# Latent-attention scores of a three-part block: the non-rotary product of each head made from rounded high parts and remainders instead of full float32 operands

## The chip, the cores and the metric

The kernel runs on one core of one Trainium2 chip. Its time is the device time of one execution in microseconds (us). The four compute engines named below are TensorE (PE; its weight loads are listed as PEld), VectorE (DVE), ScalarE (ACT) and GpSimd (POOL). SyncE (SP) only issues transfers here.

## The reference, cut to what matters

Two layers of a first block are followed by one layer of a second block, all in float32, for 256 tokens of width 2048. In each of the two layers a normed input is multiplied by `w_in` and split. Of the parts, `q_lat` (512 wide) is normed and multiplied by `w_uq`, `kv_lat` (256 wide) is normed and multiplied by `w_ukv`. For each of 8 heads this gives a query of 128 plain and 64 rotary columns, a key of 128 plain columns (the 64 rotary ones are shared by the heads) and a value of 128 columns. Then

```python
q = concatenate([q[..., :128], apply_rope(q[..., 128:], cos, sin)])
k = concatenate([k_nope, broadcast(k_pe)])
sc = einsum('bqhd,bkhd->bhqk', q, k) * 192 ** -0.5
p = softmax(sc); o = einsum('bhqk,bkhd->bqhd', p, v)
```

The rest of the layer is a gated short convolution, an attention of 4 heads over 256 memory tokens, a SiLU gate over all three, the product with `w_o`, a norm and a residual sum. The second block is a modulated Fourier mix and a squared-ReLU network of width 8192. The change touches only the product of the plain 128 columns of `q` and `k`.

## The kernel before, in words

**Two kinds of product.** Every large product is made from three rounded products. A float32 weight is split by ACT into a rounded high part (`whi`, type float32r, `split_hi`, L449 to L456) and by DVE into the remainder (`wlo`, `split_lo`, L458 to L463); the activations are kept in the same two parts, and PE adds high by high, high by remainder and remainder by high into PSUM (`fm_half`, `tm_half`, `ukv_half`, `pair_of`). All matmuls are written by `mm` at L467. The smaller products (scores, probabilities by values) have plain float32 operands in the kernel before, the rotary part of the MLA scores excepted: that has a rounded query of which both 64-row halves, high part and remainder, stand in one tile `qr`, against `krh` and `krl`.

**Steps.** The weights of a layer come in 1 MB units, and one half of a unit is a step; a layer has 144 steps. A step of a group is what PE does with one `whi` and one `wlo` tile. The groups in order are: memory keys and values (steps 0 to 15), `qlat` (16 to 23), `kvlat` (24 to 31), `gc` (32 to 39), four groups `uq` of two heads each and of 2 steps each (40 to 47), four groups `ukv` likewise (48 to 55), `xin` (2 groups of 4 steps, 56 to 63), `gb`, `qmem`, eight of `gate`, four of `wo`. Below, "uq2" is the third group of `uq`.

**Order on the engines.** PE, ACT and DVE each run through the steps in a fixed order of their own. At step s, ACT first rounds the weights of step s + 3 (AHEAD = 3), and DVE first makes their remainder. DVE next does one unit of the `w_mod` sum (L1160) where the plan of `mod_slots` has one: in this stretch at steps 43, 47, 50, 53 and from 57 on. Then both engines take the results of the group that PE has just ended out of PSUM (`ended`, ACT from L796, DVE from L1235). That is done at the step that follows the group's last: uq0 at step 42, uq3 at 48, ukv0 at 50, ukv3 at 56.

**Accumulators.** There are two PSUM accumulators of 1024 columns, used by turns (`acc_of`). The first matmul of a group therefore waits until the group two before it has been taken out: on the count `acc_act` for groups that ACT reads and `acc_dve` for those in the list `DVE_READS` (L82; PE waits from L1775 on).

**A group of `uq` before.** Columns 0 to 511 of the accumulator are the plain parts of two heads, columns 512 to 767 the rotary parts. ACT copies the rotary columns in four pieces to `swap` (L825), then the plain ones to `O` (L827), then rounds the rotary part of the previous group (`rotary_hi`, L794, L795; for uq0 the shared key part, L792). DVE multiplies the rotary columns by the cosines (the last time that it reads the accumulator, and where `acc_dve` is counted), then `swap` by the sines, adds the two, and makes the remainder of the previous group's rotary part (`rotary_lo`).

**A group of `ukv` before.** ACT copies the values to `V` (L830) and the plain keys of two heads to `kn` (L835). DVE does nothing with the accumulator; at ukv0 it makes the last rotary remainder.

**Scores.** Head h is scored before PE's share of step 59 + 3h (`QK_AT`). For each of two blocks of 128 queries, PE issues one float32 matmul `O` by `kn`, then `qr` by `krh` and `qr` by `krl`. The maximum, the exponential, the transposes and the product with the values follow at this and the next six steps, on DVE, ACT and PE.

**Memory.** `swap` lies at A + 38 KB, inside the 8 KB of `kn` (A + 32). So ACT waits, before it writes the keys of ukv3, until DVE has finished with `swap` (L833).

The lines that cause the wait at the head of a group:

```python
of = max(g - 2, 0)
if of in ACT_READS:
    pe.wait_ge(acc_act, act_reads(l, of))
if of and of in DVE_READS:
    pe.wait_ge(acc_dve, dve_reads(l, of))
```

Of the kernel before, what the change touches and what calls it, by code (L numbers as in the profile page):

```python
# [5 lines left out]
F32 = mybir.dt.float32  # L6
# [63 lines left out]
def acc_of(g):  # L70

    return (g + 1) % 2
# [6 lines left out]


ACT_READS = [g for g in range(NG) if GROUPS[g][1] != "FP"]
DVE_READS = [g for g in range(NG) if GROUPS[g][0] in ("mem", "uq", "wo") or GROUPS[g][1] == "FP"]  # L82
PAIRED = [g for g in range(NG) if GROUPS[g][1] == "FP"]


# [166 lines left out]
def build_program(nc, x, memt, positions, small, w_in, w_uq, w_ukv, w_mk, w_mv, w_o, post_g,  # L252
# [3 lines left out]
    with ctx:  # L256
        origin = nc.sbuf_base + (-nc.sbuf_base) % 64

        def at(name, shape, kb, dt=F32):
            return nc.alloc_sbuf_tensor_at(name, shape, dt, offset=origin + int(kb * 1024))  # L260
# [26 lines left out]
        csx = at("csx", [P, MT, SEQ], A + 36)  # L287
        otok = at("otok", [P, MT, D], A + 12)
        qpe = at("qpe", [P, HEADS // 2, SEQ], A + 28)
        kn = at("kn", [P, HEADS, SEQ], A + 32)  # L290
        qn = at("qn", [P, MT, QL], A + 32)
        kvn = at("kvn", [P, MT, KVL + 2 * ROPE], A + 36)
        swap = at("swap", [P, SEQ], A + 38)


        qr = at("qr", [P, HEADS, SEQ], 32, F32R)
# [422 lines left out]
        def _(act):  # L719
# [77 lines left out]
            def ended(act, l, g):  # L797

                name = GROUPS[g][0]
                a = acc[acc_of(g)]  # L800
                i = g - G_OF[name]
                act.wait_ge(half_used, l * LH + H_AT[g + 1])
                if name == "mem":
                    for t in range(MT):
                        factor = sc[:, RS + t:RS + t + 1] if l else 1.0
                        w = nc.scalar.activation(mv[:, t, :], a[:, t * 512:(t + 1) * 512], ACT.Copy, scale=factor)
                    w.then_inc(acc_act, 1)
                if name in ("qlat", "kvlat"):
                    w, n = (0, QL) if name == "qlat" else (1, KVL)
                    for t in range(MT):  # L810
                        i = nc.scalar.activation(sqlat[:, t, 0:n], a[:, t * 512:t * 512 + n], ACT.Square, scale=n ** -0.5,
                                                 accum_out=sc[:, LS + 2 * w + t:LS + 2 * w + t + 1])
                    i.then_inc(lat[w]["ss"], 1)
                if g in PAIRED:
                    if name == "gate" and i >= 2:
                        act.wait_ge(x_sum, 8 * l + i - 1)
                    if name == "qmem":
                        act.wait_ge(conv_out, 2 * l + i + 1)
                    nc.scalar.activation(xhalf[acc_of(g)][:, :, :], a.rearrange("p (t e n) -> p t e n", t=2, e=2)[:, :, 1, :],
                                         ACT.Copy).then_inc(x_copied, 1)  # L820
                if name == "uq":

                    act.wait_ge(rope_out, l * 5 + i + 1)
                    for b in range(4):
                        w = nc.scalar.activation(swap[32 * b:32 * b + 32, :], a[32 * (b ^ 1):32 * (b ^ 1) + 32, 512:768], ACT.Copy)  # L825
                    w.then_inc(swap_in, 1)
                    nc.scalar.activation(flat(O[:, 2 * i:2 * i + 2, :]), a[:, 0:512], ACT.Copy).then_inc(acc_act, 1)  # L827
                    rotary_hi(l, i)
                if name == "ukv":
                    nc.scalar.activation(V[:, :, 256 * i:256 * i + 256],  # L830
                                         a[:, 512:1024].rearrange("p (t n) -> p t n", t=MT), ACT.Copy)
                    if i == 3:

                        act.wait_ge(rope_out, l * 5 + 5)
                    nc.scalar.activation(flat(kn[:, 2 * i:2 * i + 2, :]), a[:, 0:512], ACT.Copy).then_inc(acc_act, 1)  # L835
                    if i == 0:
                        rotary_hi(l, 4)
                if name == "wo":
                    row_squares([a[:, t * 512:(t + 1) * 512] for t in range(MT)], i)
                    act.wait_ge(row_sq, 2 * (4 * l + i) + 2)  # L840
                    act.sem_inc(acc_act, 1)
# [235 lines left out]
        def _(dve):  # L1077
# [147 lines left out]
            def rotary_lo(l, i):  # L1225
# [6 lines left out]
                    w = tt(qr[0:64, 2 * i - 1, :], qpe[64:128, i - 1, :], qr[64:128, 2 * i - 1, :].bitcast(F32), ALU.subtract)  # L1232
                w.then_inc(rope_lo, 1)

            def ended(l, g):  # L1235
                name = GROUPS[g][0]
                a = acc[acc_of(g)]
# [5 lines left out]
                if name == "uq":  # L1243
                    dve.wait_ge(swap_in, 5 * l + i + 2)
                    o = qpe[:, i, :]
                    tt(o, a[:, 512:768], cosT[:, :], ALU.mult).then_inc(acc_dve, 1)
                    tt(swap[:, :], swap[:, :], sinT[:, :], ALU.mult).then_inc(rope_prod, 1)
                    dve.wait_ge(rope_prod, 5 * l + i + 2)
                    tt(o, o, swap[:, :], ALU.add).then_inc(rope_out, 1)
                    rotary_lo(l, i)  # L1250
                    dve.wait_ge(rope_out, 5 * l + i + 2)
                if g in PAIRED:
                    dve.wait_ge(x_copied, paired(l, g))
                    half = xhalf[acc_of(g)]
                    own = O[:, HEADS + 2 * (i % 2):HEADS + 2 * (i % 2) + 2, :]
# [324 lines left out]
        def _(pe):  # L1580
# [55 lines left out]
            for l in range(DEPTH):  # L1636
                base = l * LH
                for s in range(LH if l + 1 < DEPTH else LH - 8):
# [71 lines left out]
                    for h in range(NH):  # L1710
                        n = l * NH + h + 1
                        b = h % 2
                        mem_head = h - HEADS
                        if s == QK_AT[h]:
                            if h == 0:
                                pe.wait_ge(acc_act, act_reads(l, G_OF["xin"] - 1))
                                pe.wait_ge(rope_lo, l * 5 + 5)
                                pe.wait_ge(lat[1]["lo"], l + 1)
                            if h == HEADS:
                                pe.wait_ge(keys_scaled, 1)  # L1720
                                pe.wait_ge(values_scaled, 1)
                                pe.wait_ge(acc_dve, dve_reads(l, G_OF["qmem"] + 1))
                            if h >= 2:
                                pe.wait_ge(exp_ready, n - 2)
                            for t in range(MT):
                                tok = slice(t * P, (t + 1) * P)
                                o = M[b][:, t * SEQ:(t + 1) * SEQ]
                                if h < HEADS:
                                    mm(o, O[:, h, tok], kn[:, h, :], True, False)
                                    mm(o, qr[:, h, tok], krh[:, :], False, False)  # L1730
                                    i = mm(o, qr[:, h, tok], krl[:, :], False, True)
                                else:
                                    i = mm(o, O[:, h + CT, tok], mkT[:, mem_head, :], True, True)
                            i.then_inc(S_ready, 1)
# [252 lines left out]
```

## Time and profile before

| | us |
|---|---|
| median of 3 runs | 1673.34 |
| lowest and highest | 1671.97, 1675.25 |
| the profiled execution, its own time | 1673.14 |
| span of that execution in the trace | 1671.3 |
| PE busy in the span | 1658.4 |
| DVE busy in the span | 1193.5 |
| ACT busy in the span | 858.0 |

The execution takes 1.8 us more than its span. Busy time of an engine is the union of its instructions' intervals. A matmul's interval reaches from its start to its modelled end, and the next one starts long before that end, so the distance of two starts is what a matmul costs PE, not its duration. Times in the timeline are counted from the start of the span.

### The profile page before, as it was taken

What the parts mean: (1) busy time and instruction counts of PE and PEld (TensorE: products, weight loads), DVE (VectorE), ACT (ScalarE), POOL (GpSimd) and SP (SyncE); (2) the same over time, 40 slices, a digit from 0 to 9 for tenths busy, and PEclk for the clock granted to TensorE, in tenths of its full rate; (3) what the DMA queues carried; (4) which work ended last, traced back from release to release, by engine and by line L of the source; (5) the groups of instructions that cost most, each with busy time, mean ns of one, the idle gap of its engine ahead of it and who ended that gap; (6) DMA issues with size and microseconds to landing.
All of it is one profiled execution on the core that took longest, in us unless ns stands there. A gap on an engine that the chain in (4) does not pass through costs nothing.

```text
span 1671.3 us, 22298 instructions
## 1 busy us (share of the span) xinstructions
PE 1658.4 (99%) x8949; PEld 1433.7 (86%) x8949; DVE 1193.5 (71%) x1299; ACT 858.0 (51%) x1212; POOL 25.0 (1%) x42
## 2 busy tenths in 40 slices
PE   9999999999999999999999999999999999999997
PEld 8899888888989888888888888888888888888886
DVE  7878778897877877789688678776654556546655
ACT  7667556444646655644464554434443344334442
POOL 0000000000100000000000000000000000000000
PEclk9999999999999999999999999999999999999999
DMA  9689687997678867699649478887555665666553
GB/s 335 215 277 303 221 268 242 320 362 275 243 255 265 283 210 269 227 346 370 218 153 360 150 231 297 290 289 248 180 188 190 198 181 199 213 190 192 186 201 126
DMA packets 218535, 408.15 MB, mean 244 GB/s; under 512 B 9376, under 2 KB 87744, under 8 KB 217664
## 3 DMA queue, kind: packets, MB, share of 16 engines
q1 hardware_dynamic: 217936, 404.58, 71.3%
q10 hardware_dynamic: 496, 2.14, 0.3%
q8 instruction: 71, 1.16, 0.3%
q14 instruction: 32, 0.26, 0.1%
HBM read 404.58 MB, written 2.11 MB: 243 GB/s over the span
## 4 chain that ended last, share of the span: by engine, by line
PE 95%; DMA 1%; issue 1%; DVE 1%; ACT 1%; SPq 0%; POOL 0%; DVEq 0%; POOLq 0%; ACTq 0%
PE banks L467 94%; DMA raw<-in_w_mv 1%; PE banks L1707 1%; PE banks L1669 0%; DMA raw<-in_w_in 0%; DVE wlo L463 0%; ACT whi L456 0%; PE banks L1678 0%; DVE X L1121 0%; DVE X L1576 0%; SPq L611 0%; SPq L596 0%; SPq L595 0%; PE banks L1864 0%; POOL sc L685 0%
## 5 line engine op out<-in xcount | busy, mean ns | idle before, releaser
L463 DVE TENSOR_TENSOR wlo<-raw,whi 128x1024 fp32r<-128x1024 f32 (+2 forms) x561 | 663.5, 1189 | 373.1 <-ACT whi L456 370.3
L456 ACT ACTIVATE whi<-raw 128x1024 fp32r<-128x1024 f32 (+2 forms) x561 | 573.0, 1030 | 578.6 <-PE banks L467 522.2
L467 PE MATMUL banks<-H,whi 128*128 128x512 f32 x2048 | 660.0, 398 | 1.7 <-ACT kn L835 1.0
L467 PEld LDWEIGHTS banks<-H,wlo 128*128 128x128 f32 x2048 | 384.9, 188 | 88.5
L467 PE MATMUL banks<-whi,Y 128*128 128x512 f32 x1472 | 455.7, 389 | 0.0
L467 PE MATMUL banks<-H,wlo 128*128 128x256 f32 x2048 | 402.6, 278 | 0.0
L467 PEld LDWEIGHTS banks<-whi,Y 128*128 128x128 f32 x1472 | 276.3, 188 | 57.3
L467 PEld LDWEIGHTS banks<-H,whi 128*128 128x128 f32 x2048 | 317.0, 189 | 3.1 <-ACT kn L835 1.4
L467 PE MATMUL banks<-wlo,Y 128*128 128x512 f32 x768 | 298.8, 389 | 0.0
L1160 DVE SCALAR_TENSOR_TENSOR modacc<-modw,cvx,modacc 128x1024 f32<-128x1024 f32 x188 | 240.5, 1279 | 13.8 <-DMA modw<-in_w_mod 13.6
L467 PEld LDWEIGHTS banks<-wlo,Y 128*128 128x128 f32 x768 | 144.2, 188 | 30.0
L467 PE MATMUL banks<-whi,H 128*128 128x512 f32 (+1 forms) x480 | 140.3, 370 | 0.1
L467 PEld LDWEIGHTS banks<-whi,H 128*128 128x128 f32 x480 | 87.7, 188 | 14.2 <-issue 0.5
L467 PE MATMUL banks<-wlo,H 128*128 128x512 f32 (+1 forms) x256 | 94.5, 369 | 0.0
L467 PEld LDWEIGHTS banks<-wlo,H 128*128 128x128 f32 x256 | 48.1, 188 | 7.2
L918 ACT ACTIVATE prob<-banks,sc 128x256 f32<-128x256 f32 x48 | 22.4, 471 | 58.0 <-DVE sc L1346 58.0
L1063 ACT ACTIVATE Y<-sqr 128x1024 fp32r<-128x1024 f32 x16 | 17.0, 1061 | 44.4 <-DVE sqr L1545 44.4
L685 POOL TENSOR_TENSOR sc<-sc 128x1 f32<-128x1 f32 (+1 forms) x18 | 13.2, 735 | 1465.3 <-DVE sc L1572 713.1
L467 PE MATMUL banks<-memh,whi 128*128 128x256 f32 x128 | 34.8, 287 | 0.2
L467 PE MATMUL banks<-memh,wlo 128*128 128x256 f32 x128 | 34.2, 283 | 0.0
L467 PE MATMUL banks<-meml,whi 128*128 128x256 f32 x128 | 34.2, 283 | 0.0
L972 ACT ACTIVATE prob<-prob,sc 128x256 f32<-128x256 f32 x48 | 21.9, 503 | 23.1 <-DVE sc L1350 23.1
(225 smaller groups left out, 1338.4 us busy)
## 6 DMA issues: line engine op xcount, KB each, us to landing
modw<-in_w_mod SPq DMA_DIRECT2D x192, 512.0 KB, 6.5
raw<-in_w_in SPq DMA_DIRECT2D x72, 1024.0 KB, 5.4
raw<-in_w_mlp_in SPq DMA_DIRECT2D x64, 1024.0 KB, 5.6
raw<-in_w_mlp_out SPq DMA_DIRECT2D x64, 1024.0 KB, 5.0
raw<-in_w_o SPq DMA_DIRECT2D x32, 1024.0 KB, 6.6
raw<-in_w_fnet SPq DMA_DIRECT2D x16, 1024.0 KB, 6.8
raw<-in_w_mv SPq DMA_DIRECT2D x7, 1024.0 KB, 6.4
raw<-in_w_mk SPq DMA_DIRECT2D x6, 1024.0 KB, 6.1
```

Of the source, the lines that this page charges most:

```text
L456: nc.scalar.activation(hi_part(step, n), raw[u % RAW][:, (step % 2) * n:(step % 2) * n + n], ACT.Copy).then_inc(hi_ready, 1)
L463: nc.vector.tensor_tensor(wlo[u % RAW][:, part], raw[u % RAW][:, part], hi_part(step, n).bitcast(F32), ALU.subtract).then_inc(lo_ready, 1)
L467: return nc.tensor.matmul(o, a, b, start=start, stop=stop, skip_group_check=True)
L685: nc.gpsimd.tensor_tensor(sc[:, r0:r0 + n], sc[:, m0:m0 + n], sc[:, POW:POW + n], ALU.pow).then_inc(done, 1)
L918: w = nc.scalar.activation(prob[:, b, t, :], M[b][:, t * SEQ:(t + 1) * SEQ], ACT.Exp, scale=scale, bias=sc[:, NM + 2 * b + t:NM + 2 * b + ...
L972: w = nc.scalar.activation(prob[:, b, t, :], prob[:, b, t, :], ACT.Copy, scale=sc[:, RINV + 2 * b + t:RINV + 2 * b + t + 1])
L1063: nc.scalar.activation(Yhi[:, 4 * j:4 * j + 4, :], sqr[:, :, :], ACT.Copy).then_inc(m_hi, 1)
L1160: nc.vector.scalar_tensor_tensor(modacc[:, :], modw[j % MRING][:, :], co, modacc[:, :], ALU.mult, ALU.add).then_inc(mod_used, 1)
L1707: i = nc.tensor.transpose(M[2][:, kt * SEQ + t * P:kt * SEQ + (t + 1) * P], prob[:, b, t, kt * P:(kt + 1) * P], ident[:, :])
```

## The change

The plain query and key parts are no longer kept as float32 (`O`, `kn`) but as rounded high part and remainder (`qhi`, `qlo`, `khi`, `klo`). ACT's two copies out of PSUM become copies to `qhi` and `khi`, of the same size. DVE subtracts, for each of the eight groups of `uq` and `ukv` in a layer, the high part from the accumulator (`rest_of`), and only then counts the accumulator as read; `ukv` joins `DVE_READS`. PE makes the plain product of a head from three rounded matmuls. `swap` moves to an address that overlaps nothing else in use then, and the wait at L833 goes. The diff, whole but for the blank context:

```diff
-DVE_READS = [g for g in range(NG) if GROUPS[g][0] in ("mem", "uq", "wo") or GROUPS[g][1] == "FP"]
+DVE_READS = [g for g in range(NG) if GROUPS[g][0] in ("mem", "uq", "ukv", "wo") or GROUPS[g][1] == "FP"]

-        kn = at("kn", [P, HEADS, SEQ], A + 32)
+        qhi = at("qhi", [P, HEADS, SEQ], A + 12, F32R)
+        qlo = at("qlo", [P, HEADS, SEQ], A + 32, F32R)
+        khi = at("khi", [P, HEADS, SEQ], 40, F32R)
+        klo = at("klo", [P, HEADS, SEQ], 48, F32R)
-        swap = at("swap", [P, SEQ], A + 38)
+        swap = at("swap", [P, SEQ], 56)

 # ACT, ended(), name == "uq"
-                    nc.scalar.activation(flat(O[:, 2 * i:2 * i + 2, :]), a[:, 0:512], ACT.Copy).then_inc(acc_act, 1)
+                    nc.scalar.activation(flat(qhi[:, 2 * i:2 * i + 2, :]), a[:, 0:512], ACT.Copy).then_inc(acc_act, 1)
 # name == "ukv"
-                    if i == 3:
-                        act.wait_ge(rope_out, l * 5 + 5)
-                    nc.scalar.activation(flat(kn[:, 2 * i:2 * i + 2, :]), a[:, 0:512], ACT.Copy).then_inc(acc_act, 1)
+                    nc.scalar.activation(flat(khi[:, 2 * i:2 * i + 2, :]), a[:, 0:512], ACT.Copy).then_inc(acc_act, 1)

 # DVE
+            def rest_of(l, g, lo, hi, i):
+                dve.wait_ge(acc_act, act_reads(l, g))
+                two = slice(2 * i, 2 * i + 2)
+                tt(flat(lo[:, two, :]), acc[acc_of(g)][:, 0:512], flat(hi[:, two, :]).bitcast(F32), ALU.subtract).then_inc(acc_dve, 1)
 # ended(), name == "uq"
-                    tt(o, a[:, 512:768], cosT[:, :], ALU.mult).then_inc(acc_dve, 1)
+                    tt(o, a[:, 512:768], cosT[:, :], ALU.mult)
                     tt(swap[:, :], swap[:, :], sinT[:, :], ALU.mult).then_inc(rope_prod, 1)
                     dve.wait_ge(rope_prod, 5 * l + i + 2)
                     tt(o, o, swap[:, :], ALU.add).then_inc(rope_out, 1)
+                    rest_of(l, g, qlo, qhi, i)
                     rotary_lo(l, i)
                     dve.wait_ge(rope_out, 5 * l + i + 2)
+                if name == "ukv":
+                    rest_of(l, g, klo, khi, i)

 # PE, at the first scores and in each head
                                 pe.wait_ge(acc_act, act_reads(l, G_OF["xin"] - 1))
+                                pe.wait_ge(acc_dve, dve_reads(l, G_OF["xin"] - 1))
-                                    mm(o, O[:, h, tok], kn[:, h, :], True, False)
+                                    mm(o, qhi[:, h, tok], khi[:, h, :], True, False)
+                                    mm(o, qhi[:, h, tok], klo[:, h, :], False, False)
+                                    mm(o, qlo[:, h, tok], khi[:, h, :], False, False)
                                     mm(o, qr[:, h, tok], krh[:, :], False, False)
```

## Rows read from the trace of the kernel before

**Rows 1.** The page: busy time of PE, and its granted clock in 40 slices.

```profile
PE 1658.4 (99%) x8949; PEld 1433.7 (86%) x8949; DVE 1193.5 (71%) x1299; ACT 858.0 (51%) x1212; POOL 25.0 (1%) x42
...
PEclk9999999999999999999999999999999999999999
```

**Rows 2.** Stretches from uq to the first scores, both layers: length, PE, PEld, DVE, ACT, POOL, clock, DMA.

```profile
118.80:155.40 36.60, 35.71 (x272) 34.08 (x271) 30.30 (x45) 29.62 (x55) 0.00 (x0) 1.00 0.84 283
532.60:569.30 36.70, 35.63 (x273) 34.14 (x272) 30.36 (x45) 29.56 (x55) 0.00 (x0) 1.00 0.83 282
```

**Rows 3.** Timeline of PE around the first head: start and duration in us.

```profile
155.17 0.40 PE L467 MATMUL banks<-H,whi 128*128 128x512 f32 x1
...
155.40 0.59 PE L467 MATMUL banks<-kn,O 128*128 128x256 f32 x2
...
156.73 0.40 PE L467 MATMUL banks<-H,whi 128*128 128x512 f32 x1
```

**Rows 4.** Timeline of PE in uq0: the first and last of 40 consecutive matmuls.

```profile
119.73 0.28 PE L467 MATMUL banks<-qlh,wlo 128*128 128x256 f32 x1
...
124.42 0.28 PE L467 MATMUL banks<-qlh,wlo 128*128 128x256 f32 x1
```

**Rows 5.** Groups by shape: DVE's 512-column operation that reads PSUM, and ACT's two.

```profile
L1079 DVE TENSOR_TENSOR O<-banks,xhalf 128x512 f32<-128x512 f32 x1 | 0.7, 684 | 0.0
...
L827 ACT ACTIVATE O<-banks 128x512 f32<-128x512 f32 x4 | 2.4, 599 | 0.1
```

**Rows 6.** Timeline of PE where groups follow each other: last of the old, first of the new.

```profile
125.13 0.28 PE L467 MATMUL banks<-qlh,wlo 128*128 128x256 f32 x1
...
129.46 0.28 PE L467 MATMUL banks<-qlh,wlo 128*128 128x256 f32 x1
...
136.66 0.28 PE L467 MATMUL banks<-whi,kvl 128*128 128x256 f32 x1
137.23 0.36 PE L467 MATMUL banks<-kvh,whi 128*128 128x256 f32 x1 [0.29 <-ACT O L827]
...
142.94 0.28 PE L467 MATMUL banks<-whi,kvl 128*128 128x256 f32 x1
143.59 0.36 PE L467 MATMUL banks<-kvh,whi 128*128 128x256 f32 x1 [0.37 <-DVE wlo L463]
...
146.41 0.28 PE L467 MATMUL banks<-whi,kvl 128*128 128x256 f32 x1
146.92 0.50 PE L467 MATMUL banks<-H,whi 128*128 128x512 f32 x1 [0.23 <-ACT kn L835]
...
560.76 0.50 PE L467 MATMUL banks<-H,whi 128*128 128x512 f32 x1 [0.79 <-ACT kn L835]
```

**Rows 7.** Timeline of DVE in layer 0, from the end of uq0 to xin.

```profile
124.50 0.42 DVE L1079 TENSOR_TENSOR qpe<-qpe,swap 128x256 f32<-128x256 f32 x1
124.84 0.42 DVE L1079 TENSOR_TENSOR krl<-kr,krh 128x256 fp32r<-128x256 f32 x1
...
129.10 0.42 DVE L1079 TENSOR_TENSOR qpe<-qpe,swap 128x256 f32<-128x256 f32 x1
...
136.71 0.42 DVE L1079 TENSOR_TENSOR qpe<-banks,cosT 128x256 f32<-128x256 f32 x1
...
140.55 1.28 DVE L1160 SCALAR_TENSOR_TENSOR modacc<-modw,cvx,modacc 128x1024 f32<-128x1024 f32 x1 [0.42 <-DMA modw<-in_w_mod]
141.87 0.85 DVE L1079 TENSOR_TENSOR qr<-qpe,qr 64x256 fp32r<-64x256 f32 x2
142.75 1.29 DVE L463 TENSOR_TENSOR wlo<-raw,whi 128x512 fp32r<-128x512 f32 x2
...
147.32 1.22 DVE L463 TENSOR_TENSOR wlo<-raw,whi 128x1024 fp32r<-128x1024 f32 x1
```

**Rows 8.** Timeline of ACT in layer 0: the last copy of uq3.

```profile
136.38 0.60 ACT L827 ACTIVATE O<-banks 128x512 f32<-128x512 f32 x1
```

**Rows 9.** Groups by shape: the 20 warm-up matmuls at the start of the span.

```profile
L467 PE MATMUL banks<-warm 128*128 128x256 f32 x20 | 4.4, 407 | 1.2 <-DVE warm L1180 1.2
```

## The prediction

> **What bounds the kernel now.** I read the page first. PE is busy for 99% of the span at full clock [rows 1], so a microsecond added to or taken from PE's sequence is a microsecond of the kernel. DVE has 29% idle over the whole, which says nothing about one stretch. So I cut out, in both layers, what lies between the start of the `uq` groups and the first scores [rows 2]: 36.6 us, in which DVE is busy for 30.3 us (83%) and ACT for 29.6 us. DVE has 6.3 us left, and what matters is whether its new work lies in those holes or ahead of something that PE waits for. Last I read the timeline of PE at the borders of groups. The reader is to see that three of them already stall in layer 0: from 136.66 to 137.23, 142.94 to 143.59 and 146.41 to 146.92 [rows 6], where the pace of a 256-column matmul is (124.42 - 119.73) / 39 = 0.120 us [rows 4]. Here PE waits for ACT and DVE, not they for PE.
>
> The first stall is worth a second look. Its row names ACT's copy, which ended at 136.38 + 0.60 = 136.98 [rows 8]. PE waits there for DVE's cosine product too, and that ended at 136.71 + 0.42 = 137.13 [rows 7]. PE started 0.10 us after the latter. So an accumulator's release by DVE counts already.
>
> **Term 1, the scores.** Between the last 512-column matmul of step 58 (155.17) and the first of step 59 (156.73) lie 1.56 us [rows 3]. 0.23 of it is the first one's own (155.40 - 155.17), which leaves 1.33 for a head, 0.665 for each block of 128 queries. Two of its matmuls are the rounded rotary ones at 0.120 each [rows 4], so the float32 one costs about 0.425. After the change it is three rounded ones of the same shape, 0.360. The saving is 0.065 x 2 blocks x 8 heads x 2 layers = 2.1 us. ACT's copies keep their size and cost nothing more.
>
> The Trainium skill (FP8 and Floating Point Precision, TensorE Precision Notes) says that a true float32 product takes four passes through the array. With each pass at the row's 0.120 that would be 0.480 and a saving of 3.8 us. The row has 0.425, near four passes of a slightly shorter pass, so the measured 2.1 us stays in the sum.
>
> **Term 2, DVE's subtractions.** There are 8 in a layer, 512 columns from PSUM, 0.68 us each by the nearest row [rows 5]; the next instruction of DVE starts 0.08 before the end of the one ahead (124.84 against 124.92 [rows 7]), so each takes 0.60 of the queue: 4.8 us a layer, against 6.3 us idle. But `acc_dve` now comes after it, and it waits for ACT's copy. I follow layer 0 border by border. PE loses (release - start of the old group's last matmul) + 0.08; that is what the stall at 137.23 gives: 137.13 - 136.66 + 0.07 = 0.54.
>
> - uq2, waiting for uq0: the addition stands at 124.50 to 124.92; the subtraction takes the place at 124.84 and ends at 125.52. PE's last start is 125.13 [rows 6]. Loss 0.46.
> - uq3, waiting for uq1: DVE comes 0.53 later, so the addition of 129.10 [rows 7] ends at 130.05 and the subtraction at 130.65. PE's last start is 129.46 + 0.46 = 129.92. Loss 0.81, lag of PE 1.27.
> - ukv0, waiting for uq2: the two remainders of uq2's step are short ones, the subtraction ends at about 134.5, before PE's 133.78 + 1.27. Loss 0.
> - ukv1, waiting for uq3: ACT's copies to `swap` move with PE, DVE's product goes from 136.71 to 137.7, the addition ends at 138.9, the subtraction at 139.5. PE's last start is 136.66 + 1.27 = 137.93. Loss 1.65 in place of 0.54. Lag 2.4.
> - ukv2, waiting for ukv0: behind that subtraction stand two rotary remainders (0.85), two weight remainders (1.29), the `w_mod` unit (1.28) and two more rotary remainders (0.85) [rows 7]; then the subtraction, which ends at 144.4. PE's last start of ukv1 is now 137.23 + 23 x 0.120 = 140.0 [rows 4, 6], and becomes 142.4. Loss 2.0, where there was none. Lag 4.4.
> - ukv3: it stalled for a weight remainder (143.59, 0.6 us lost [rows 6]). That remainder, the next in DVE's queue, is there at 145.1, while PE arrives at 147.4. The old loss goes: lag 3.8.
> - xin0, waiting for ukv2: the transfer of its weights starts when ukv0 ends and moves with PE. DVE then has a remainder (1.22), a `w_mod` unit (1.28), a remainder (1.22) [rows 7] and the subtraction, which ends at 151.7 against PE's last start of 146.41 + 3.8 = 150.2. Loss 1.5 in place of 0.5. Lag 4.8.
>
> From here on a step has eight matmuls of 512 columns and eight of 256, 8 x (0.23 + 0.12) = 2.8 us [rows 3, 4]; the next border (xin1) is four of them away and the remainders are three steps ahead, so DVE's lag is covered. The new wait ahead of the first scores is for the subtraction of ukv3, which ends two remainders and one subtraction after 151.7, near 154.8; the scores come at 160.
>
> Layer 1 has the same order and the same `w_mod` slots. Its stall at ukv3 is missing and the one at xin0 is larger (560.76 [rows 6], 0.9 lost), so 0.46 + 0.81 + 1.1 + 1.9 + 0.5 = 4.8. Term 2 is +9.6 us.
>
> **Edits at no cost.** The wait that goes (L833) is never the last: the addition of uq3 is done 1.2 us after the start at 136.71 [rows 7], and ukv3 itself ends later than ukv2, whose successor starts PE at 143.59 [rows 6]. The new addresses of `swap`, `khi` and `klo` add no wait, because their old users ended in step 22 (`msq`) or in the layer before. No DMA is added. SP stands behind DVE's `w_mod` units for its next `w_mod` load only; if those came late, the weights queued behind them would, and I keep 1 us of the range for it.
>
> **The sum.** -2.1 + 9.6 = +7.5 us on the execution's own 1673.14: 1680.6. That execution lies 0.2 below the median, so 1680.8.
>
> **The bounds.** The score term lies between 0 (each rounded matmul at a third of 0.425) and -4.1 (each at 0.107, the 256 columns of a pass as 0.425 / 4 gives it, with the rotary ones too: 5 x 0.107 = 0.53 for 0.665). The subtraction term lies between 6 us (if the order at ukv2 and xin0 is kinder by one hidden `w_mod` unit a layer, and something of uq3's) and 16 x 0.68 = 10.9 us plus 1 us of late weights. Together 1675.2 to 1685.2, both ends at once being unlikely: 1676 to 1685.
>
> **The rivals.**
>
> *A. DVE's holes take the work in.* DVE has 6.3 us idle for 4.8 us. If PE did not stall more than now, only term 1 would be left: 1673.3 - 2.1 = 1671.2, no slower. For it: the whole-kernel share of 71%. Against it: the release at 137.13 that PE already waits for [rows 6, 7], with the subtraction coming after it by the order of the code. It decides if less than 5.5 us of the 9.6 appear, since 0.2%, 3.3 us, is about what a measurement of this kernel tells from no change. Chance 0.09, of which 0.02 beyond 0.2% faster (with the full 4.1 us on the scores).
>
> *B. The clock falls in the longer stalls.* It is 1.00 in both stretches with pauses up to 1.06 us between starts [rows 2, 6]; the new ones reach 2 us. A fall at each of the four longest a layer and a rise like that of the warm-up, where 20 matmuls took 4.4 us [rows 9] for 2.4 at full pace, would cost 2 us each: some 16 us more, 1696. The Trainium skill (TensorE: Matmul & The Clock Gate, What's actually happening) has activity as what keeps the clock up; the trace agrees so far as it goes, with no fall in 1671 us. Chance 0.03.
>
> *C. The remainders become the bound of PE.* If DVE's lag at step 56 did not die out before the scores, whose reduction, exponential and transposes share its queue, each of the eight heads could wait again. Against it: PE's steps take 2.8 us there, DVE's work in one is a remainder and a `w_mod` unit, 1.22 + 1.28 [rows 7]. With 2 us more a layer: 1685. Chance 0.08.
>
> The forecast keeps 0.80. Slower by over 0.2%: 0.80 + 0.03 + 0.08 = 0.91; within 0.2%: 0.07; faster: 0.02.
>
> **What would show it.** PE's starts at uq2, uq3, ukv1, ukv2 and xin0 come 0.5 to 2 us after the last of the group before, each just behind a 0.68 us DVE operation from PSUM, named in the row or found beside it. The first scores start near 160.1 instead of 155.4, and a head takes 1.20 us instead of 1.33. DVE gains 10.9 us busy, ACT none. If ukv2 starts on time, the order that I wrote down for DVE is wrong; if a head takes 1.33, term 1 is; if the first scores of layer 0 come at 155.4, rival A holds.

## The result and the profile after

| | before | after |
|---|---|---|
| median, us (6 runs each) | 1673.55 | 1682.12 |
| lowest and highest | 1671.97, 1675.25 | 1681.48, 1682.79 |
| profiled execution, its own time | 1673.14 | 1682.79 |
| its span | 1671.3 | 1681.0 |

The ratio is 1.0050 with a 95% interval of 1.0040 to 1.0061, so the change costs 8.6 us (0.5%); the two profiled executions are 9.7 us apart. The forecast was 1680.8 in a range of 1676 to 1685.

The page of the changed kernel, its busy times and the granted clock:

```profile
PE 1660.3 (99%) x8981; PEld 1436.4 (85%) x8981; DVE 1202.2 (72%) x1315; ACT 858.7 (51%) x1212; POOL 25.0 (1%) x42
...
PEclk9999999999999999999999999999999999999999
```

PE is busy only 1.9 us more and the span is 9.7 us longer. That is the mark of waiting. DVE is busy 8.7 us more, where the forecast said 10.9 by 16 durations; the 0.08 us that each overlaps its neighbour explains 1.3 of the 2.2, and the rest stays open. To find where, I took the start of the last matmul of every step in both traces and subtracted. This is TensorE's lag; what it gains at a border is what that border costs. In us:

| border | forecast | layer 0 | layer 1 |
|---|---|---|---|
| uq2 | 0.46 | 0.42 | 0.42 |
| uq3 | 0.81 | 0.69 | 0.67 |
| ukv0 | 0 | 0 | 0 |
| ukv1 (above the old stall) | 1.1 | 1.32 | 1.35 |
| ukv2, first step | 2.0 | 3.24 | 2.43 |
| ukv2, second step | 0 | 0.39 | 1.12 |
| ukv3 | -0.6, 0 | -0.59 | 0.00 |
| xin0 (above the old stall) | 1.0, 0.5 | 0.60 | -0.57 |
| eight heads | -1.05 | -1.05 | -1.05 |

The borders sum to 6.1 and 5.4 us where 4.8 was forecast for each; the heads give back 2.1. Outside this stretch the lag changes by 0.3 us in all. The stretches of [rows 2], from uq to shortly before the first scores:

```profile
119.10:161.40 42.30, 37.21 (x270) 35.32 (x269) 35.17 (x53) 29.82 (x55) 0.00 (x0) 0.96 0.76 255
537.90:579.60 41.70, 37.22 (x270) 35.32 (x270) 35.38 (x53) 29.84 (x55) 0.00 (x0) 0.96 0.76 256
```

They end 0.3 and 0.4 us ahead of where those of [rows 2] ended in PE's work, and so are 5.7 and 5.0 us longer where the table has 6.1 and 5.4. DVE is busy 4.9 and 5.0 us more, ACT as long as before. And the mean granted clock, 1.00 before, is 0.96. The page can't show that: a digit of it covers 42 us. The timeline of PE at the borders, which answers to [rows 6], with two rows from inside ukv2:

```profile
125.37 0.28 PE L470 MATMUL banks<-qlh,wlo 128*128 128x256 f32 x1
125.86 0.36 PE L470 MATMUL banks<-qlh,whi 128*128 128x256 f32 x1 [0.21 <-issue]
...
130.12 0.28 PE L470 MATMUL banks<-qlh,wlo 128*128 128x256 f32 x1
130.86 0.35 PE L470 MATMUL banks<-qlh,whi 128*128 128x256 f32 x1 [0.46 <-issue]
...
139.92 0.36 PE L470 MATMUL banks<-kvh,whi 128*128 128x256 f32 x1 [1.64 <-issue]
...
142.74 0.28 PE L470 MATMUL banks<-whi,kvl 128*128 128x256 f32 x1
144.93 0.55 PE L470 MATMUL banks<-kvh,whi 128*128 128x256 f32 x1 [1.91 <-ACT khi L835]
145.28 0.41 PE L470 MATMUL banks<-kvl,whi 128*128 128x256 f32 x1
145.49 0.41 PE L470 MATMUL banks<-kvh,wlo 128*128 128x256 f32 x1
...
153.27 0.47 PE L470 MATMUL banks<-H,whi 128*128 128x512 f32 x1 [0.87 <-issue]
```

And the timeline of DVE, which answers to [rows 7]:

```profile
125.08 0.68 DVE L1079 TENSOR_TENSOR qlo<-banks,qhi 128x512 fp32r<-128x512 f32 x1
...
130.07 0.68 DVE L1079 TENSOR_TENSOR qlo<-banks,qhi 128x512 fp32r<-128x512 f32 x1
...
139.13 0.68 DVE L1079 TENSOR_TENSOR qlo<-banks,qhi 128x512 fp32r<-128x512 f32 x1
...
141.94 1.28 DVE L1160 SCALAR_TENSOR_TENSOR modacc<-modw,cvx,modacc 128x1024 f32<-128x1024 f32 x1
143.25 0.85 DVE L1079 TENSOR_TENSOR qr<-qpe,qr 64x256 fp32r<-64x256 f32 x2
144.14 0.69 DVE L1079 TENSOR_TENSOR klo<-banks,khi 128x512 fp32r<-128x512 f32 x1
...
152.49 0.68 DVE L1079 TENSOR_TENSOR klo<-banks,khi 128x512 fp32r<-128x512 f32 x1
```

Lay the two beside each other. Each subtraction ends at 125.76, 130.75, 139.81, 144.83 and 153.17, and PE starts 0.10 to 0.11 us after each. The names in the PE rows mislead: "issue" at four of five, and at ukv2 ACT's copy to `khi`. TensorE waits there for ukv0's copy, which had ended at 141.20; the one that ended at 144.71 is ukv1's, and TensorE does not wait for it here (experiment 4 shows it). Ask which group the wait is for, and look for an end 0.1 us ahead of the start.

The matmuls after 144.93 are 0.21 us apart in place of 0.12. The granted clock in the middle of ukv2, after it, and in the same place of layer 1:

```profile
139.80:144.90 5.10, 3.10 (x24) 2.93 (x25) 4.95 (x10) 4.34 (x9) 0.00 (x0) 1.00 0.95 320
144.90:147.40 2.50, 2.47 (x11) 2.50 (x12) 1.73 (x3) 0.00 (x0) 0.00 (x0) 0.50 0.91 302
...
563.70:569.50 5.80, 5.74 (x35) 5.77 (x36) 4.18 (x5) 2.10 (x3) 0.00 (x0) 0.71 0.51 173
```

0.50 is the lower of the clock's two levels, 1.2 GHz for 2.4. The trace's record of the clock has it at 0.5 from 144.9 for 3.4 us and from 564.8 for 3.4 us, and nowhere else before the end. Ahead of the first, TensorE had been idle for 1.64 us at ukv1 and 1.91 us at ukv2, by the rows above; ahead of the second for 1.66 and 1.92 us. The Trainium skill (TensorE: Matmul & The Clock Gate, What's actually happening) has activity as what releases the throttle, and here the trace agrees, in that both falls come behind the longest idle times of the stretch.

The head, in the timeline of PE, answers to [rows 3]:

```profile
161.48 0.40 PE L470 MATMUL banks<-H,whi 128*128 128x512 f32 x1
161.71 0.28 PE L470 MATMUL banks<-khi,qhi 128*128 128x256 f32 x1
161.83 0.28 PE L470 MATMUL banks<-klo,qhi 128*128 128x256 f32 x1
...
162.90 0.40 PE L470 MATMUL banks<-H,whi 128*128 128x512 f32 x1
```

1.42 us less the 0.23 of the first is 1.19 for ten rounded matmuls, against 1.33. The first scores start at 161.71, where about 160.1 was forecast: 0.24 of the difference was there before the stretch, 1.2 is the fall of the clock.

### The profile page after: what moved, and what is told of

It is laid out like the page before. It is cut to its first block, busy times and chain, and to the rows that moved or that the text cites. A ratio compares the mean times of both kernels' runs of the same rounds, so it can differ in the third digit from the quotient of the medians.

```text
span 1681.0 us, 22392 instructions
## 1 busy us (share of the span) xinstructions
PE 1660.3 (99%) x8981; PEld 1436.4 (85%) x8981; DVE 1202.2 (72%) x1315; ACT 858.7 (51%) x1212; POOL 25.0 (1%) x42
## 3 DMA queue, kind: packets, MB, share of 16 engines
HBM read 404.58 MB, written 2.11 MB: 242 GB/s over the span
## 4 chain that ended last, share of the span: by engine, by line
PE 96%; issue 1%; ACT 1%; DVE 0%; DMA 0%; SPq 0%; POOL 0%; DVEq 0%; POOLq 0%; ACTq 0%
PE banks L470 95%; PE banks L1716 1%; PE banks L1678 0%; DMA raw<-in_w_mv 0%; PE banks L1687 0%; DVE X L1121 0%; ACT whi L459 0%; ACT swap L828 0%; DVE X L1585 0%; SPq L599 0%; SPq L598 0%; PE banks L1876 0%; POOL sc L688 0%; ACT junk L731 0%; DVE wlo L466 0%
```

## The experiments

The theory is that all of the loss is the place of the subtractions in VectorE's queue, ahead of what TensorE waits for, with the clock's fall behind the longest stall. The rivals are the score matmuls, ScalarE's copies, and that VectorE has too little time in any order. All diffs are against the changed kernel, unless said otherwise. Each time is compared with the kernel before on the same chip.

**1. The scores alone.** The remainders are neither made nor used, and three matmuls of the high parts stand for a head's plain product. `ukv` leaves `DVE_READS`, `acc_dve` is counted at the cosine product again:

```diff
-                    rest_of(l, g, qlo, qhi, i)
-                if name == "ukv":
-                    rest_of(l, g, klo, khi, i)
-                                    mm(o, qhi[:, h, tok], klo[:, h, :], False, False)
-                                    mm(o, qlo[:, h, tok], khi[:, h, :], False, False)
+                                    mm(o, qhi[:, h, tok], khi[:, h, :], False, False)
+                                    mm(o, qhi[:, h, tok], khi[:, h, :], False, False)
```

> The changed kernel without VectorE's subtractions: no remainders of the plain parts are made, the accumulators are released as in the kernel before, and each head still has three rounded matmuls in place of the float32 one (the high parts three times, so the two remainder products are left out of the result). Theory (the three products save 2.1 us, and all of the loss comes from the subtractions): 1671.4 us, 2.1 below the kernel before; a head takes 1.20 us on TensorE for 1.33; the first scores of layer 0 start at about 155.2 us as before. Rival (the rounded matmuls or their weight loads cost what was lost): 1682 us, or at least above 1674.

Measured: 1671.09 against 1672.94 us, ratio 0.9988 (0.9979 to 0.9997). The heads take 1.05 us less in each layer. The change's own gain on TensorE is real. The first head in the timeline of PE:

```profile
155.61 0.40 PE L470 MATMUL banks<-H,whi 128*128 128x512 f32 x1
155.84 0.52 PE L470 MATMUL banks<-khi,qhi 128*128 128x256 f32 x3
...
157.03 0.40 PE L470 MATMUL banks<-H,whi 128*128 128x512 f32 x1
```

**2. The remainders alone.** They are made and not used.

```diff
-                                    mm(o, qhi[:, h, tok], khi[:, h, :], True, False)
-                                    mm(o, qhi[:, h, tok], klo[:, h, :], False, False)
-                                    mm(o, qlo[:, h, tok], khi[:, h, :], False, False)
+                                    mm(o, qhi[:, h, tok].bitcast(F32), khi[:, h, :].bitcast(F32), True, False)
```

> The changed kernel with all its subtractions, but the plain product of a head made by one float32 matmul of the high parts, as long as the one before (the remainders are made and not used). Theory: 1682.1 + 2.1 = 1684.2 us, with the same stalls at uq2, uq3, ukv1, ukv2 and xin0 and the granted clock at half for 3.4 us in each layer. Rival (the loss is in the scores): 1673.5 us.

Measured: 1684.18 against 1672.94 us, ratio 1.0065 (1.0050 to 1.0080). The two halves of the change are -1.9 and +11.2 us, each against its own runs of the kernel before; their sum, 9.4, lies between the 8.6 of the changed kernel's medians and the 9.7 of its trace. One part of the expectation failed: the clock, read behind the stall at ukv2 in both layers, fell in the second only.

```profile
145.00:150.00 5.00, 4.75 (x39) 4.78 (x40) 3.84 (x6) 2.64 (x5) 0.00 (x0) 1.00 0.82 261
562.50:568.00 5.50, 4.11 (x22) 4.14 (x23) 3.30 (x7) 2.23 (x4) 0.00 (x0) 0.69 0.80 270
```

Both stalls were 2.19 us from start to start. So the fall is possible there and not certain. In layer 0, with the clock up and nothing filled in, the borders cost 4.88 us for the 4.8 forecast.

**3. Filling the stall.**

```diff
+                    if first and g == G_OF["ukv"] + 2:
+                        for _ in range(14):
+                            mm(M[2][:, 0:SEQ], kvh[:, 0, 0:P], kvh[:, 0, :], True, True)
                     if first and g > 1:
```

> The changed kernel with 14 matmuls of 256 columns on idle data, 1.7 us, issued by TensorE ahead of its wait at ukv2 in both layers, where it stands still for 2.1 us. No wait is shortened. Theory (the half clock after that stall, 3.4 us in each layer, is caused by the stall and costs 1.2 to 1.6 us a layer): the granted clock stays at 1.00 and the time falls to about 1679.2 us. Rival (the slow pace of steps 52 and 53 comes from something else than the standstill, or the stall only grows by what is filled in): 1682.1 us or more, with the clock at 0.5 as before.

Measured: 1681.09 against 1672.94 us, ratio 1.0048 (1.0033 to 1.0063). The timeline of PE in layer 0, and the clock behind it in both layers:

```profile
143.12 1.84 PE L470 MATMUL banks<-kvh 128*128 128x256 f32 x14
145.18 0.36 PE L470 MATMUL banks<-kvh,whi 128*128 128x256 f32 x1 [0.23 <-ACT khi L835]
```

```profile
145.00:150.00 5.00, 4.82 (x40) 4.85 (x41) 3.85 (x6) 2.68 (x4) 0.00 (x0) 1.00 0.79 252
562.70:567.70 5.00, 4.84 (x40) 4.87 (x41) 3.84 (x6) 2.70 (x4) 0.00 (x0) 1.00 0.71 215
```

The clock stays up, and TensorE is no later at ukv2 for the filling (from 143.00 to 145.18 are 2.18 us, where the stall had 2.19). The lag that the borders make is 4.86 and 4.83 us in the two layers: the forecast 4.8 of each. Against the changed kernel's 6.07 and 5.43 the falls cost 1.2 and 0.6 us. At ukv2 itself a fall costs 1.5 us (sixteen matmuls 0.21 us apart in place of 0.12); part of it comes back, because TensorE then arrives later at xin0, where it waits anyway (0.60 and -0.57 in the table, for 0.87 and 0.32 here). By the medians it is 8.2 us above the kernel before, where the changed kernel is 8.6 above: a gain of 0.4 to 1.0 us, less than the 2.9 expected and less than the 1.8 of the traces. How often the clock falls in executions without a trace is not known. Their mean granted clock is on record: 0.997 in three of the changed kernel's six and 0.998 in the other three, which are the three fastest, and 0.998 or 0.999 in the four of this experiment. Two falls make 0.002, so some executions of the changed kernel probably had fewer. That filling keeps the clock up is not proved by two layers either: without it the clock fell behind the stall at ukv2 in four of six (both layers of the changed kernel, one each in experiments 2 and 6).

**4. One subtraction moved.**

```diff
-                if name == "ukv" and i == 0:
-                    rotary_lo(l, 4)
...
                     rest_of(l, g, klo, khi, i)
+                    if i == 0:
+                        rotary_lo(l, 4)
```

> The changed kernel with one thing moved: VectorE makes ukv0's subtraction ahead of the last two rotary remainders (0.85 us) in place of behind them, at step 50. Theory (TensorE waits at ukv2 for the place of the subtraction in VectorE's queue): the start of ukv2 comes 0.85 us earlier, 1.7 us in both layers, and if the shorter stall of 1.1 us leaves the clock up, another 2.4 to 3.2 us: 1677.2 to 1680.4 us. Rival (TensorE waits there for ScalarE's copy to khi, which the row names, or for a weight remainder): no change, 1682.1 us.

Measured: 1680.08 against 1672.94 us, ratio 1.0040 (1.0026 to 1.0054). The three runs with a mean clock of 0.999 took 1678.9 to 1680.1, the two with 0.997 and 0.998 took 1681.2. At ukv2 TensorE starts 1.19 us after the last matmul in place of 2.19, in both layers. The queue's order decides there, and the copy that the row names does not. In layer 0 the microsecond won was lost again at xin0, where the gap grew from 1.15 to 2.11 us and the clock fell behind it. VectorE's subtraction again ended 0.1 us before TensorE's start at 151.76, but the chain that leads to it began with a transfer: ScalarE had waited for the weights of xin0, as the timeline of ACT shows. In order, the timelines of PE and ACT, and the clock:

```profile
143.94 0.35 PE L470 MATMUL banks<-kvh,whi 128*128 128x256 f32 x1 [0.91 <-issue]
...
151.76 0.47 PE L470 MATMUL banks<-H,whi 128*128 128x512 f32 x1 [1.83 <-issue]
```

```profile
146.41 2.00 ACT L459 ACTIVATE whi<-raw 128x1024 fp32r<-128x1024 f32 x2 [1.67 <-DMA raw<-in_w_in]
```

```profile
152.00:156.00 4.00, 4.00 (x16) 3.43 (x16) 2.69 (x3) 1.61 (x3) 0.00 (x0) 0.57 1.07 371
```

In layer 1 the clock stayed at 1.00, and the lag of the stretch is 3.81 us, 1.0 below that of experiment 3.

**5. Less of VectorE's other work.** The `w_mod` units of steps 47, 50, 53 go to 91, 98, 119.

```diff
-HEAVY = ({21, 24, ...
+HEAVY = ({47, 50, 53, 21, 24, ...
-         | set(range(64, 69)) | {72, 77, 84, 91, 98, 119, 126, 133}
+         | set(range(64, 69)) | {72, 77, 84, 126, 133}
```

> The changed kernel with VectorE's w_mod units at steps 47, 50 and 53 of both layers moved to steps 91, 98 and 119; all the work is still done. Theory (TensorE waits for the place of the subtraction in VectorE's queue): nothing changes at uq2, uq3 and ukv1; at ukv2 the stall is 1.2 us shorter, at xin0 the subtraction ends 1.2 us earlier, and the granted clock stays at 1.00. The lag of TensorE at step 56 is about 3.3 us a layer in place of 5.4 to 6.1: 1677.5 us. Rival (ScalarE's copies or the weights' transfers set the borders, VectorE's load does not matter): 1682 us.

Measured: 1679.67 against 1672.89 us, ratio 1.0038 (1.0025 to 1.0052). In the stretch it did more than expected: the lag of the borders is 2.6 us in each layer, with the clock at 1.00. But at step 128 of layer 0, where TensorE sums the first quarter of `w_mod`, 2.0 us were lost: VectorE's last unit was late, and the clock fell for 3.4 us at 382.8. So the time missed the expected 1677.5. The timelines of DVE and PE there:

```profile
375.71 1.28 DVE L1160 SCALAR_TENSOR_TENSOR modacc<-modw,cvx,modacc 128x1024 f32<-128x1024 f32 x1 [3.58 <-DMA modw<-in_w_mod]
```

```profile
379.58 1.92 PE L470 MATMUL banks<-sel,modacc 128*128 128x4 f32 x16 [0.24 <-DVE modacc L1160]
```

VectorE was not short of time there: it had waited 3.58 us for the load of a unit. And this fall has no long stall ahead of it, only 0.24 us and sixteen matmuls of 4 columns, 1.8 us long; the kernel before has the sixteen at 376.55, without the wait and without a fall. The moved work had become a new wait 230 us later.

**6. Subtracting while ScalarE copies.** In the four uq groups ScalarE copies the plain parts first.

```diff
 # ACT
+                    nc.scalar.activation(flat(qhi[:, 2 * i:2 * i + 2, :]), a[:, 0:512], ACT.Copy).then_inc(q_rounded, 1)
                     act.wait_ge(rope_out, l * 5 + i + 1)
                     for b in range(4):
...
-                    nc.scalar.activation(flat(qhi[:, 2 * i:2 * i + 2, :]), a[:, 0:512], ACT.Copy).then_inc(acc_act, 1)
+                    act.wait_ge(swap_in, 5 * l + i + 2)
+                    act.sem_inc(acc_act, 1)
 # DVE
+                    dve.wait_ge(q_rounded, 4 * l + i + 1)
+                    tt(flat(qlo[:, two, :]), a[:, 0:512], flat(qhi[:, two, :]).bitcast(F32), ALU.subtract)
                     dve.wait_ge(swap_in, 5 * l + i + 2)
...
-                    tt(o, a[:, 512:768], cosT[:, :], ALU.mult)
+                    tt(o, a[:, 512:768], cosT[:, :], ALU.mult).then_inc(acc_dve, 1)
...
-                    rest_of(l, g, qlo, qhi, i)
```

> The changed kernel with another order in the four uq groups: ScalarE copies the plain parts ahead of the four pieces of swap, VectorE subtracts while ScalarE makes those, and the cosine product is again the last reading of the accumulator. Theory (the loss at uq2, uq3 and ukv1 comes from the subtraction standing behind the whole rotary chain): the losses 0.42 and 0.69 us at uq2 and uq3 vanish, the one at ukv1 falls from 1.9 to about 1.2 us, 1.8 us a layer; ukv2 still stalls by 2 us, with or without the half clock: 1677.5 to 1679.5 us. Rival (VectorE has too little time in the stretch in any order, so what is won early is lost at ukv2 and xin0): 1681.5 us or more.

Measured: 1682.40 against 1672.89 us, ratio 1.0054 (1.0039 to 1.0068); the profiled execution took 1680.93. The losses at uq2 and uq3 fell from 1.1 to 0.1 us together, that at ukv1 stayed at 1.34, and the one at ukv2 grew from 2.1 to 2.9 us (3.4 in layer 1, where the clock fell behind it). The rival was right. From 132.9 to 146.0 us VectorE is busy for 12.80 of 13.10 us; the row of PE below it is the stall of layer 0, the longest idle time in any of these traces, behind which the clock stayed up:

```profile
132.90:146.00 13.10, 8.77 (x72) 8.42 (x71) 12.80 (x24) 10.03 (x21) 0.00 (x0) 1.00 0.76 260
```

```profile
144.36 0.35 PE L470 MATMUL banks<-kvh,whi 128*128 128x256 f32 x1 [2.70 <-ACT khi L837]
```

What order wins at the first borders is waited for at the later ones. So the theory needed its second half: order and load. In these 13 us three subtractions, the weights' remainders, the rotary chain and two `w_mod` units leave VectorE no room.

**7. Only the queries' subtractions.** The keys' remainders are not made and are left out of the result; `ukv` leaves `DVE_READS` as in experiment 1.

```diff
-                if name == "ukv":
-                    rest_of(l, g, klo, khi, i)
-                                    mm(o, qhi[:, h, tok], klo[:, h, :], False, False)
+                                    mm(o, qhi[:, h, tok], khi[:, h, :], False, False)
```

> The changed kernel with the subtractions of uq alone: the remainders of the keys are not made, and the high parts of the keys stand in their place in the result. Theory (each border has its own loss): 0.42 + 0.69 + 1.32 us of lag a layer as in the changed kernel at uq2, uq3 and ukv1, nothing new at ukv2 and xin0, and the old stall at ukv3 of layer 0 gone; with 2.1 us less in the scores 1675 to 1676 us, and no fall of the clock. Rival (ukv2 and xin0 are late because of the load that uq leaves on VectorE's queue, not because of their own subtractions): 1678 us or more.

Measured: 1674.90 against 1673.24 us, ratio 1.0009 (1.0000 to 1.0018). The losses are 0.42 + 0.69 + 1.35 us in layer 0, nothing at ukv2 (the lag is 2.56 at steps 50 to 53), and the clock stays up. Four of the eight subtractions of a layer cost 2.46 us at their own borders, of which 0.7 to 1.1 us come back at ukv3 and xin0, whose old stalls vanish. The other four bring the rest, and the clock fell only where they were made: behind 1.65 us of idle time at ukv1 alone it stayed up in both layers.

**8. All rearrangements together.** Experiments 4, 5 and 6, and at steps 54 and 56 both engines take the accumulator out before they make the weights' two parts:

```diff
+EARLY = (54, 56)
...
                 for s in range(LH):
+                    if s in EARLY:
+                        ended(act, l, ENDED[s])
                     if base + s + AHEAD < stage_end(base + s):
                         split_hi(act, base + s + AHEAD)
```

> The changed kernel with all four rearrangements: uq's subtraction ahead of the rotary chain, ukv0's ahead of the rotary remainders, the w_mod units of steps 47, 50 and 53 moved to 91, 98 and 119, and at steps 54 and 56 ScalarE and VectorE take the accumulator out before they make the weights' two parts. The computation is the changed kernel's. Theory (all of the loss is order on VectorE and ScalarE, TensorE's own part of the change saves 2.1 us): the stalls at uq2, uq3, ukv2 and xin0 are gone, ukv1 keeps about what it has in the kernel before, the clock stays at 1.00: 1670 to 1672 us, 1 to 3 us below the kernel before. Rival (4.8 us of new work a layer can't be hidden beside 36.6 us of TensorE): 1675 us or more.

Measured: 1675.08 against 1672.89 us, ratio 1.0011 (1.0002 to 1.0021), five of ten runs at 1672.4 to 1674.3 and five at 1675.9 to 1677.2. The time is the rival's and not the expected 1670 to 1672, but the rival's reason, work that can't be hidden in the stretch, is not in the trace. In the stretch the theory held: the borders cost 0.15 us in layer 0 and 0.12 in layer 1, and what stalls remain are 0.95 us at ukv1 and 0.78 at ukv2 from start to start. 2.4 us were lost at step 128 of layer 0, the place of experiment 5 (VectorE had waited 3.53 us for a load, TensorE 0.56 us for VectorE), with the clock at 0.79 in the mean:

```profile
376.00:384.00 8.00, 7.44 (x35) 6.24 (x35) 5.16 (x7) 4.06 (x7) 0.00 (x0) 0.79 0.97 369
```

**9. The same with the kernel before.** The diff of `HEAVY` and of `EARLY`, on the kernel before.

> The kernel before with the two rearrangements that it can take: the same w_mod units moved, and at steps 54 and 56 the accumulator taken out before the weights' parts. It tells how much of the time of the rearranged changed kernel is owed to the change. Theory: its three stalls of 0.5 to 0.9 us at ukv3 and xin0 go, the one at ukv1 stays: about 1.5 to 2 us below the kernel before, 1671.3 us, so that the rearranged changed kernel is within 1 us of it. Rival (those stalls are set by the transfer of the weights of xin0): no change, 1673.3 us.

Measured: 1672.74 against 1672.89 us, ratio 1.0004 (0.9994 to 1.0013), seven runs from 1671.2 to 1674.0 and three from 1675.8 to 1677.2, these with a mean clock of 0.996 or 0.997. The trace, of the run at 1671.25, has TensorE 1.3 us earlier after each stretch: the three old stalls at ukv3 and xin0 went, as expected. The median does not show it: 1671.3 was expected.

**10 and 11. The units at steps 84, 91 and 98** in both rearranged kernels, and not at 119.

```diff
-         | set(range(64, 69)) | {72, 77, 84, 91, 98, 119, 126, 133}
+         | set(range(64, 69)) | {72, 77, 119, 126, 133}
```

> The same rearranged changed kernel as e9_all_early, but with the three w_mod units at steps 84, 91 and 98 and not at 119, so that the first w_mod sum at step 128 is no longer met late. Theory (2.0 to 2.4 us of e5_no_mods and e9_all_early were lost at step 128 of layer 0, to a late w_mod unit and the clock's fall behind that stall): the lag that e9_all_early shows from step 128 of layer 0 on is gone, the time is about 1671 to 1672 us, 1 to 2 us below the kernel before. Rival (that loss has to do with the wo stage itself): 1675 us as e9_all_early.

> The rearranged kernel before, e10_before_early, with its three w_mod units at the same steps 84, 91 and 98. Theory: 1670.5 to 1671.5 us, and 0 to 1 us below the rearranged changed kernel, so that the change doesn't pay even with its subtractions well placed. Rival (in a well placed form the 2.1 us of the scores show in full): the rearranged changed kernel is 1 to 2 us faster than this one.

Measured: the changed kernel 1672.64 us, ratio 0.9999 (0.9990 to 1.0008); the kernel before 1672.28 us, ratio 0.9994 (0.9985 to 1.0003). The loss at step 128 is gone from the trace, and the two are level with each other and with the kernel before. Both lie above what was expected (1671 to 1672 and 1670.5 to 1671.5 us). The stalls that the changed one keeps, in the timeline of PE:

```profile
137.76 0.35 PE L471 MATMUL banks<-kvh,whi 128*128 128x256 f32 x1 [0.69 <-ACTq L833]
...
141.37 0.36 PE L471 MATMUL banks<-kvh,whi 128*128 128x256 f32 x1 [0.51 <-issue]
```

In both traces about 1 us went at a third place, a wait of TensorE near 759 us for a small row that VectorE makes at step 114 of layer 1.

**12. The second sum at its old step.**

```diff
-            if (18 <= s < 139 and s not in HEAVY or l and s in (3, 6, 7)) and ...
+            if (18 <= s < 139 and s not in HEAVY or l and s in (3, 6, 7, 13, 14, 17)) and ...
```

> The rearranged changed kernel e11_all_84 with three more w_mod units at steps 13, 14 and 17 of layer 1, so that the second w_mod sum stands again at step 63 of that layer, as in the kernel before, and not at step 73. Theory (each layer of the rearranged changed kernel is 0.9 us shorter than before, and 1 us of it was given back near 758 us to the row that follows the late sum): 1671.4 us, 1.8 us below the kernel before, so ahead of both kernels. Rival (the added units make VectorE late ahead of layer 1's first products, or the row is late for another reason): 1672.6 us or more, no faster than before.

Measured: 1672.37 against 1672.97 us, ratio 0.9994 (0.9985 to 1.0003). The theory failed: the sum is at its old step, and the wait at the row is still there:

```profile
759.47 0.28 PE L1759 MATMUL banks<-ident,R 128*16 128x128 f32 x1 [0.88 <-DVE R L1084]
```

VectorE itself is late for the row. The timeline of DVE shows where it falls behind:

```profile
734.74 1.28 DVE L1165 SCALAR_TENSOR_TENSOR modacc<-modw,cvx,modacc 128x1024 f32<-128x1024 f32 x1 [1.44 <-DMA modw<-in_w_mod]
```

It waits 1.44 us for the load of a `w_mod` unit. In experiments 9, 10 and 11 that wait is 0.56, 1.17 and 1.58 us, and TensorE loses 0.5, 1.0 and 1.1 us at the row; in the kernel before and in experiment 1 there is neither. So the moved units seem to make a load late and not the queue longer; this was not tried apart. No version was measured faster than the kernel before beyond its interval, the one without remainders (experiment 1) excepted.

## Why the prediction was right

**The sign and the size** held: +7.5 us forecast, +8.6 by the medians, within the range. In the traces it is +9.7; without the clock's 1.8 and the 0.3 from outside the stretches 7.6 are left. Rival A, that VectorE's holes take the work in, fell with experiment 2: 11.2 us of loss for 9.6 us of added queue time (16 times 0.60).

**Term 1** (-2.1 us) was right three times: 1.19 us for a head, 1.05 us a layer in the lag, and 1.9 us by the medians of experiment 1. The four-pass price that would have saved 3.8 us did not show.

**Term 2** was right border by border, and where the clock was kept up by filling (experiment 3), right in its sum: 4.86 and 4.83 us for 4.8. That the sum is so close is in part luck, since its errors cancel: uq3 came out 0.1 us cheaper than worked out, xin0 0.1 to 0.2 cheaper, ukv2 0.1 to 0.2 dearer (2.13 in both layers of experiment 3). Within it uq2 and ukv3 came as worked out. ukv1 was 0.2 us dearer, because the `w_mod` unit and a remainder stood ahead of uq3's chain and delayed the cosine product to 138.01, where 137.7 had been written. The price of a subtraction (0.68 by the row, 0.684 in the trace) was exact. TensorE started 0.10 to 0.11 us after its end, and the rule of 0.08 us gave losses within 0.05 us of the measured ones.

**What was mis-sized** is the clock. The sum left it out, and rival B had it as something that comes at all of the four longest stalls for 2 us each, 16 us in all. In the traced execution it came once in a layer, for 3.4 us at half, and cost 1.2 and 0.6 us net. The step that failed is "It is 1.00 in both stretches with pauses up to 1.06 us between starts": a pause twice as long had no row, and its cost was taken for nothing in the sum. Nor is "no fall in 1671 us" quite so: the clock of the kernel before is at 0.50 from 1667.4 us to the end of the span, 4.6 us after the end of the last matmul. The fall comes in some executions and not in others, so its place was in the range, by up to one fall a layer.

**The edits at no cost** cost nothing that the trace shows; rival C did not come either: the lag falls from head to head and rises nowhere after xin0.

## What to carry to other kernels

Idle time of an engine over a stretch says whether work fits; whether it delays others is told by what stands behind it in the queue and by who waits for its end. Count the operations between the event and the release, border by border, and the loss can be forecast, here to 0.25 us a border, as long as the clock stays up. And when work is moved out of a crowded stretch, follow it to where it goes: here it met a sum 230 us later and cost 2.0 to 2.4 us there.

## What the runs showed that was not expected

- The clock fell to 0.50 for 3.41 us, in the changed kernel behind 1.64 us of idle time at ukv1 and 1.91 us at ukv2; the same two left it up in layer 0 of experiment 2, and 1.64 and 2.70 us left it up in layer 0 of experiment 6. In experiment 4 it fell at xin0, behind 1.83 us. In all, seven unfilled stalls held over 1.8 us of idle time, and the clock fell behind five. In experiments 5 and 8 it fell at step 128, with 0.24 and 0.56 us of idle time and sixteen matmuls of 4 columns ahead of it.
- With fourteen idle matmuls ahead of a wait it stayed up in both layers, and they delayed nothing.
- A row names the right line and the wrong group (ACT `khi` of ukv1, where the wait is for ukv0's, done 3.7 us before the start), or "issue", where the trace has an operation of another engine that ended 0.1 us before.
